# Splitting Q and K after the transpose, and the first projection in two passes

## What is computed

```python
def modulate(x, g, shift, scale):
    return rms_norm(x, g) * (1.0 + scale) + shift

sh1, sc1, gt1, sh2, sc2, gt2 = modulation(c, w_ada, b_ada)  # silu(c) @ w_ada + b_ada, in six parts
h = modulate(x, g_pre_attn, sh1, sc1)
qa, ka, va, qb, kb, vb = attn_projections(h, w_in, g_qa, g_ka)  # qa, ka normed per head
qa, ka = rope_2d(qa, rows, cols), rope_2d(ka, rows, cols)      # latent rows only
qb, kb = rope_2d(qb, rows, cols), rope_2d(kb, rows, cols)
oa = blocked_gqa(qa, ...)             # group A: 8 heads, 2 K/V heads, all keys
ob = windowed_gqa_with_ctx(qb, ...)   # group B: 8 heads, window of 128 and a sink
x = x + gt1 * rms_norm(concat(oa, ob) @ w_out, g_post_attn)
# then router, top-k per expert, 16 experts of SwiGLU, and the second residual
```

## Time and profile before

| | |
|---|---|
| median of 3 runs | 975.97 us (975.77 to 977.18) |
| the profiled execution | 975.98 us, span 974.2 us |
| PE busy | 902.5 us (93%) |
| DVE busy | 331.5 us (34%) |
| ACT busy | 214.8 us (22%) |
| POOL busy | 129.2 us (13%) |
| moved by DMA | 267.11 MB, mean 274 GB/s |

### The profile page before, as it was taken

One profiled execution on the slowest core, in us unless ns is written; L12 is line 12 of the kernel. 1 busy time (PEld: TensorE's weight loads), 2 busy tenths in 40 slices (PEclk: granted clock), 3 DMA queues, 4 the chain that ended last, 5 costly groups with the idle time before them and its releaser, 6 DMA issues.

```text
span 974.2 us, 20099 instructions
## 1 busy us (share of the span) xinstructions
PE 902.5 (93%) x8601; PEld 447.6 (46%) x8601; DVE 331.5 (34%) x872; ACT 214.8 (22%) x509; POOL 129.2 (13%) x226
## 2 busy tenths in 40 slices
PE   3899999899899999449999999999999999999996
PEld 2445545677656555314444444444444444444441
DVE  2355533888767763631111111101110111011016
ACT  5122212666644653200000000000000000000002
POOL 1101100000000000021212121212121212120121
PEclk9999999999999999759999999999999999999999
DMA  9997440400000006929999999999999999999973
GB/s 359 336 346 259 173 173 31 180 2 1 1 1 23 23 23 251 414 101 357 366 402 392 394 398 403 393 394 398 402 393 393 401 400 392 394 401 401 384 256 156
DMA packets 77813, 267.11 MB, mean 274 GB/s; under 512 B 6392, under 2 KB 12072, under 8 KB 77768
## 3 DMA queue, kind: packets, MB, share of 16 engines
q1 hardware_dynamic: 69040, 248.53, 65.3%
q0 software_dynamic: 7088, 14.95, 6.1%
q10 hardware_dynamic: 1640, 3.01, 0.8%
HBM read 252.32 MB, written 14.16 MB: 274 GB/s over the span
## 4 chain that ended last, share of the span: by engine, by line
PE 86%; DVE 6%; DMA 3%; ACT 3%; issue 2%; POOL 1%; SPq 0%; ACTq 0%; DVEq 0%
PE ps L835 34%; PE ps L847 17%; PE ps L553 11%; PE ps L707 6%; PE ps L658 3%; PE ps L636 3%; DMA ring<-in_w_ada 3%; PE ps L622 2%; PE ps L505 2%; PE ps L570 1%; ACT ring L1131 1%; PE ps L736 1%; PE ps L684 1%; PE ps L813 1%; PE ps L892 1%
## 5 line engine op out<-in xcount | busy, mean ns | idle before, releaser
L835 PE MATMUL ps<-ring,reg 128*32 128x512 f32 x2048 | 232.1, 593 | 0.0
L847 PE MATMUL ps<-ring,reg 128*32 128x256 f32 x2048 | 124.0, 383 | 3.2 <-DVE reg L1573 2.2
L835 PEld LDWEIGHTS ps<-ring,reg 128*32 128x32 f32 x2048 | 66.6, 110 | 126.9 <-issue 116.2
L553 PE MATMUL ps<-ring,reg_qt 128*128 128x512 f32 x240 | 105.7, 594 | 0.9 <-ACT reg_qt L981 0.9
L847 PEld LDWEIGHTS ps<-ring,reg 128*32 128x32 f32 x2048 | 65.9, 111 | 71.1 <-issue 34.0
L1177 ACT ACTIVATE reg<-ps 128x256 f32<-128x256 f32 x16 | 6.2, 385 | 390.0 <-PE ps L887 390.0
L1588 DVE TENSOR_SCALAR reg<-ps,kt 128x512 f32<-128x512 f32 x15 | 11.3, 751 | 214.4 <-PE ps L835 214.4
L707 PE MATMUL ps<-ring,reg 128*128 128x512 f32 x160 | 76.1, 603 | 0.0
L553 PEld LDWEIGHTS ps<-ring,reg_qt 128*128 128x128 f32 x240 | 44.5, 190 | 53.0 <-issue 51.2
L1131 ACT ACTIVATE ring<-ps 128x640 f32<-128x640 f32 (+3 forms) x80 | 44.4, 555 | 72.8 <-PE ps L636 69.8
L835 PE MATMUL ps<-reg_qt,kt 128*32 128x512 f32 x512 | 57.9, 592 | 0.0
(11 more groups left out here) (218 smaller groups left out, 1005.2 us busy)
## 6 DMA issues: line engine op xcount, KB each, us to landing
ring<-in_w_up SPq DMA_DIRECT2D x32, 2048.0 KB
ring<-in_w_down SPq DMA_DIRECT2D x32, 2048.0 KB
ring<-in_w_gate SPq DMA_DIRECT2D x16, 2048.0 KB
reg_qt<-in_w_gate SPq DMA_DIRECT2D x16, 2048.0 KB
ring<-in_w_ada SPq DMA_DIRECT2D x12, 2048.0 KB
reg<-in_x_sample SPq DMA_DIRECT2D x8, 512.0 KB, 6.0
ring<-in_w_in SPq DMA_DIRECT2D x2, 2048.0 KB
ring<-in_w_out SPq DMA_DIRECT2D x2, 2048.0 KB
```

The lines of the kernel that those rows point to most:

```text
L553: last = pe.matmul(ps[:, i % 2, :], hT[:, c, t * P:(t + 1) * P], w[:, c, :], start=(c == 0), stop=(c == KC - 1))
L835: last = pe.matmul(o[64 * n + r:64 * n + r + 32, :], x[:, j, hf, r:r + 32], w[:, j, n * HALF:(n + 1) * HALF], start=(hf == 0 and j == 0), ...
L847: last = pe.matmul(o[32 * q:32 * q + 32, :], x[:, c % 2, c // 2, :], w[:, j, q * QUART:(q + 1) * QUART], start=(c == 0), stop=(c == KC - 1))
```

## The change

Three things, all before the second unit of the attention.

1. **Split after the transpose.** `turn_qk(k)` transposes `rot` itself (queries) or `doubled` (keys, doubled by ACT in `double_keys`), four transposes into one bank. ACT's `high_part` takes the high part out of PSUM into its place in qT or kT, DVE's `low_part` subtracts that from PSUM into its place. For queries each takes two instructions over 64 partitions: the heads of a pair lie on partitions 0 to 63 and 64 to 127, and the low part goes to the other half.
2. **Shift and scale in column halves.** Units `half` hold 512 columns of all 1024 rows. `mod_half(i)` multiplies one (32 matmuls of 128 columns), `half_columns` transposes it, `half_cols` makes columns of it for four chunks.
3. **The first projection in two passes.** `project_half(t, b)` does four of the eight chunks, into five banks (`FIRST_BANKS`), one for each tile. DVE normalises x now, and the bias of shift and scale comes in four loads of its own.

```diff
-UNITS = ([("ada", m, h) for m in (0, 1) for h in (0, 1)] + [("win", 0, 0), ("win", 1, 0)]
+MOD_HALVES = [(m, a) for a in (0, 1) for m in (0, 1)]
+UNITS = ([("half", 0, 0), ("half", 1, 0), ("win", 0, 0), ("half", 0, 1), ("half", 1, 1), ("win", 1, 0)]
          + [("ada", m, h) for m in (2, 3) for h in (0, 1)] + [("ada", 4, 0), ("win", 2, 0)]
          + [("ada", 4, 1), ("ada", 5, 0), ("ada", 5, 1)] + [("wout", 0, h) for h in (0, 1)])
-UNIT_SLOT = [1, 2, 3, 4, 5, 0, 2, 3, 4, 2, 3, 5, 4, 2, 3, 4, 5]
+UNIT_SLOT = [1, 2, 5, 3, 4, 0, 2, 3, 4, 2, 3, 5, 4, 2, 3, 4, 5]
 ADA_AFTER = {4: 2, 7: 3, 9: 4, 12: 5}
-COLS = {0: 0, 1: 1, 3: 2, 4: 3}
+COLS = {3: 2, 4: 3}
+FIRST_BANKS = [0, 1, 2, 3, 5]
...
+        def turned(k):
+            return ps[:, (6 + k % 2) if k < 4 else (5 if k % 2 else 2), :]
...
+        def parts_of(k):
             s, t = divmod(k - 1, TILES)
-            if k == 0 or s == 0:
+            if k <= TILES:
+                at = KEY_AT[-1] if k == 0 else (TOK if t == 0 else KEY_AT[t - 1])
                 for g in (0, 1):
-                    if k == 0:
-                        src = cache[:, 2 * g * P:(2 * g + 1) * P]
-                    elif t == 0:
-                        src = kv_ctx[:, 256 * g:256 * g + P]
-                    else:
-                        src = rot[:, (k - 1) % 2, g * P:(g + 1) * P]
-                    dst = split[:, b, 512 * g:512 * g + 512].rearrange("p (v r u d) -> p r v u d", v=2, r=2, u=2)
-                    yield src.rearrange("p (v d) -> p v d", v=2).unsqueeze(2).to_broadcast([P, 2, 2, DH]), dst
+                    by_kv = kT[g][:, :, at:at + P].rearrange("p (v r) n -> p r v n", r=2)
+                    yield turned(k)[:, 256 * g:256 * g + 256].rearrange("p (v n) -> p v n", v=2), by_kv[:, 0], by_kv[:, 1]
             else:
-                yield (rot[:, (k - 1) % 2, :].rearrange("p (h d) -> p h d", d=DH),
-                       split[:, b, :].rearrange("p (h r d) -> p r h d", h=HEADS, r=2))
+                here, there = slice(0, DH), slice(DH, P)
+                by_pair = qT[s - 1][:, :, t * P:(t + 1) * P].rearrange("p (c r) n -> p r c n", r=2)
+                for r in (0, 1):
+                    yield (turned(k)[here].rearrange("p (c n) -> p c n", c=PAIRS), by_pair[here, r], by_pair[there, r])
+                    here, there = there, here
...
+                if kind == "half":
+                    freed.append((mod_half_done, MOD_HALVES.index((m, h)) + 1))
+                elif kind == "ada" and h == 0:
                     n_half += 1
                     freed.append((ada_half, n_half))
                 elif kind == "ada":
...
                     for t in range(TILES):
                         src = A["x_prompt"][0] if t == 0 else A["x_sample"][0, (t - 1) * P:t * P]
                         sp.dma_start(x_in[:, t, :], src).then_inc(x_loaded[t], 16)
-                if kind == "ada":
+                if kind == "half":
+                    src = A["w_ada"][0].rearrange("(p c) n -> p c n", c=KC)[:, :, m * D + HALF * h:m * D + HALF * (h + 1)]
+                    sp.dma_start(dst.rearrange("p (c n) -> p c n", c=KC), src).then_inc(slot_in[slot_of(u)], 16)
+                    if (m, h) == (1, 1):
+                        load_win0(1)
+                        load_keys()
...
+            def mod_half(i):
+                m, a = MOD_HALVES[i]
+                if i:
+                    pe.wait_ge(mod_ready, i)
+                u = UNITS.index(("half", m, a))
+                landed(u)
+                w = unit_at(u, KC)
+                for c in range(KC):
+                    for q in range(4):
+                        last = pe.matmul(ps[32 * q:32 * q + 32, 4, 0:P], silu[:, c, :], w[:, c, q * P:(q + 1) * P],
+                                         start=(c == 0), stop=(c == KC - 1))
+                last.then_inc(mod_half_done, 1)
...
-            ada(0)
-            mod_columns(0, 0)
-            ada(1)
-            mod_columns(1, 1)
+            mod_half(0)
+            turn_x(0)
+            turn_x(1)
+            half_columns(0)
+            turn_x(2)
+            turn_x(3)
+            mod_half(1)
+            turn_x(4)
+            half_columns(1)
+            turn_x(5)
...
+            def project_half(t, b):
+                if b == 0 and t == 1:
+                    pe.wait_ge(ht_ready, 4)
+                if b == 0 and t == 2:
+                    pe.wait_ge(ht_raw, KC)
+                    pe.wait_ge(htc_raw, KC)
+                if b == 1 and t == 1:
+                    pe.wait_ge(ht_ready, KC)
+                w = unit_at(win_units[0], KC)
+                for c in range(4 * b, 4 * b + 4):
+                    if t == 0:
+                        pe.wait_ge(htc_ready, c + 1)
+                        if c % 4 == 0:
+                            pe.wait_ge(win0_in[b], 32)
+                    last = pe.matmul(projected(t), hT[:, c, t * P:(t + 1) * P], w[:, c, :],
+                                     start=(c == 0), stop=(c == KC - 1))
+                if b:
+                    last.then_inc(proj_done, 1)
+            project_half(0, 0)
+            turn_x(6)
+            project_half(1, 0)
+            turn_x(7)
+            mod_half(2)
+            project_half(2, 0)
+            half_columns(2)
+            mod_half(3)
+            project_half(3, 0)
+            half_columns(3)
+            project_half(4, 0)
...
             def turn_qk(k):
-                pe.wait_ge(split_ready, k + 1)
-                if k < 2:
-                    pe.wait_ge(htc_ready, KC)
+                if k <= TILES:
+                    pe.wait_ge(doubled_ready, k + 1)
                 else:
+                    pe.wait_ge(rot_ready, k)
+                if k == 0:
+                    pe.wait_ge(htc_raw, KC)
+                    pe.wait_ge(modcol_ready, 4)
+                if k >= 2:
                     pe.wait_ge(qkT_ready, k - 1)
-                    pe.wait_ge(qkT_act, k - 1)
-                for b in range(8):
-                    last = pe.transpose(ps[:, turned_banks(k)[b // 4], (b % 4) * P:(b % 4 + 1) * P],
-                                        split[:, k % 2, b * P:(b + 1) * P], ident[:, :])
+                for b in range(4):
+                    src = doubled[:, k % 2, :] if k <= TILES else rot[:, (k - 1) % 2, :]
+                    last = pe.transpose(turned(k)[:, b * P:(b + 1) * P], src[:, b * P:(b + 1) * P], ident[:, :])
                 last.then_inc(qk_turned, 1)
...
+            for c in range(6):
+                copy_xc(c)
+            act.wait_ge(modcol_ready, 2)
+            for c in range(4):
+                modulate_xc(c)
+            copy_xc(6)
+            copy_xc(7)
+            act.wait_ge(modcol_ready, 4)
+            for c in range(4, KC):
+                modulate_xc(c)
+            def double_keys(k):
...
+            def high_part(k):
                 act.wait_ge(qk_turned, k + 1)
-                bank = ps[:, (5 if k % 2 else 2), :].rearrange("p (b n) -> p b n", b=4)
-                s, t = divmod(k - 1, TILES)
-                if k == 0 or s == 0:
-                    at = KEY_AT[-1] if k == 0 else (TOK if t == 0 else KEY_AT[t - 1])
-                    dst = kT[0][:, :, at:at + P]
-                else:
-                    if k == TILES + 1:
-                        act.wait_ge(added_l, 16)
-                        act.wait_ge(added_c, 16)
-                        act.wait_ge(pad_cleared, 16)
-                    dst = qT[s - 1][:, 0:4, t * P:(t + 1) * P]
-                act.activation(dst, bank, ACT.Copy).then_inc(qkT_act, 1)
+                if k == TILES + 1:
+                    act.wait_ge(added_l, 16)
+                    act.wait_ge(added_c, 16)
+                    act.wait_ge(pad_cleared, 16)
+                for src, high, low in parts_of(k):
+                    last = act.activation(high, src, ACT.Copy)
+                last.then_inc(qkT_act, 1)
...
+            add_bias(0)
+            copy_x(0)
+            copy_x(1)
+            half_cols(0)
+            copy_x(2)
+            copy_x(3)
+            add_bias(1)
+            copy_x(4)
+            half_cols(1)
             dve.wait_ge(modcol_ready, 2)
-            for c in range(KC):
-                dve.wait_ge(ht_raw, c + 1)
-                dve.tensor_scalar(hT[:, c, P:TOK], hT[:, c, P:TOK], cmod[:, 1, 1, c:c + 1], cmod[:, 0, 1, c:c + 1],
-                                  ALU.mult, ALU.add).then_inc(ht_ready, 1)
+            for c in range(4):
+                modulate_x(c)
...
-                dve.wait_ge(high_ready, k + 1)
-                for src, dst in part_sources(k):
-                    last = dve.tensor_tensor(dst[:, 1].bitcast(F32R), src, dst[:, 0], ALU.subtract)
-                last.then_inc(split_ready, 1)
-            def qk_out(k):
-                dve.wait_ge(qk_turned, k + 1)
-                bank = ps[:, (6 if k % 2 else 3), :].rearrange("p (b n) -> p b n", b=4)
-                s, t = divmod(k - 1, TILES)
-                if k == 0 or s == 0:
```

(13 more changed lines are left out.)

180 lines of the change are left out of this document (109 added, 71 removed).

## The result

The changed kernel takes **1042.7 us** (median of 4 runs, 1040.9 to 1044.1), the kernel before on the same chip 976.6 us (4 runs, 975.8 to 979.5). The ratio is 1.066, 95% interval 1.064 to 1.068: **6.6% slower**, where 970.6 us was forecast. Executions of one kernel differ with the clock granted to them: over all runs of before, those with a mean granted clock of 0.981 took 975.7 to 976.9 us, those with 0.976 or 0.977 took 977.1 to 980.3.

A forecast was written before the change was run, and what follows sets the result against it. TensorE was taken to bound the kernel, so gains before the attention sweep would reach the end one for one: 8.1 - 4.7 + 3.9 - 1.9 = 5.4 us less than 975.98, so 970.6 us, range 967.6 to 974.8.

The forecast's parts named there:

- T: The end of the last projection before attention, 166.56 us in the kernel before, forecast at 159.3.
- the tail: From the last projection into attention: pieces over 64 partitions delay the first turned probabilities, T+12.2 instead of T+10.37, 1.9 us lost.
- the sweep: The attention's 80 units, where PE, VectorE and ScalarE hand score blocks on; no gain or loss of its own was forecast.
- Startup: Before the first projection: with shift and scale in halves it starts at 27.8 instead of 35.91, 8.1 us earlier.
- Rivals A: Startup: a half of shift or scale costs what a whole does, 3.6 us; +5.9, 976.5 us, no change; chance 0.13.
- C: Startup: PE stays at 1.2 GHz through the first dense half projection; +7.7, 978.3 us; 0.07 together with D's late start.
- D: Startup: smaller ada pieces load slower, second half unit 1.7 us later; up to +1.5, 972.1 us; chance 0.07.
- The new wait: First projection's second passes: PE waits 0.7 us at turn_qk(3); with added work, 4.7 of 8.1 us given back by ada(2)'s end.
- The dense stretch: From 77.53 to 166.56 us, before attention: nine turn_qk each 0.44 us shorter, 3.9 us gained on PE.
- Rival B: Attention's first units catch up, so the 1.9 us lost on the way into attention vanish; 968.7 us; chance 0.11.

The follow-up runs named there:

- after_plus24: The changed kernel with 24 more PE instructions (empty semaphore waits) ahead of its first matmul: 974.35 us, 0.9963 of the kernel before.
- after_plus72: The changed kernel with 72 already satisfied waits ahead of its first modulation half: 973.4 us, 0.9959 of the kernel before.
- split_plus24: The kernel before with only the split after the transpose, plus 24 instructions of waits to place the loop: 976.97 us, 0.9991 of the kernel before.
- tail_plus24: The changed kernel with 24 instructions of waits, last two turned tiles in banks 6 and 7, their low parts subtracted later: 969.1 us, 0.9907 of the kernel before.

## Why the prediction was wrong

**The step that failed** is in the first paragraph: "the expert loop is paced by PE, so what is won or lost before the sweep should reach the end one for one", and "the expert loop unchanged". The work in it is unchanged, its place in the program is not. I counted what the change adds and removes in time, on each engine, and never in instructions. Nothing in the page of before warned of it: 76 instructions of room were left to the limit, 131 were added, and a loop that fits shows no trace of the limit but packets that are missing.

The rest of the miss is in the sum itself: in the profiled execution T is 7.50 us earlier (7.3 forecast), the tail gives back 2.8 (1.9) and the sweep 1.0 (nothing), which is the 3.65 at the loop instead of 5.4.

The steps one by one:

- **Startup: right.** mod_half(0) starts at 16.87 (16.7) and takes 3.64 (4.2, at half speed), the next half 1.96 (2.2), the first projection starts at 27.94 (27.8). Rows of after:

```profile
16.87 3.64 PE L536 MATMUL ps<-ring,reg 128*32 128x128 f32 x64 [16.87 <-DMA ring<-in_w_ada]
...
23.84 1.96 PE L536 MATMUL ps<-ring,reg 128*32 128x128 f32 x64
...
27.94 3.70 PE L609 MATMUL ps<-ring,reg_qt 128*128 128x512 f32 x8 [0.79 <-ACT reg_qt L1059]
```

  Rivals A (halves at 3.6 us), C (the clock low until the first projection) and D (smaller pieces slower) fall by these rows: the pace rises between the 3.64 and the 1.96 of the same 64 instructions, though the granted clock reads 1.00 in both. The rule of the Trainium skill ("TensorE: Matmul & The Clock Gate", Part 3, The mechanism) that was weighed against the row gave an estimate of 3.5 us a half; 1.96 was measured, so at this shape a load does not add up with its matmul.
- **The new wait: right, and its place.** turn_qk(3) waits 0.44 us (0.7), the only one of the second passes; ada(2) ends at 73.95 (74.1).

```profile
69.78 0.66 PE L649 MATMUL ps<-ident,reg 128*128 128x128 f32 x4 [0.44 <-ACT reg L1082]
70.36 3.66 PE L557 MATMUL ps<-ring,reg 128*32 128x256 f32 x64
73.95 7.13 PE L633 MATMUL ps<-ring,reg_qt 128*128 128x512 f32 x16
80.92 0.60 PE L649 MATMUL ps<-ident,reg 128*128 128x128 f32 x4
```

- **The dense stretch: right.** turn_qk takes 0.44 us less (0.60 to 1.04), T is 159.06 (159.3).
- **The tail: right mechanism, too small.** 2.8 us and not 1.9. Two pieces over 64 partitions take 1.39 us on VectorE and 1.18 on ScalarE, where about 1.2 and 1.1 were taken; the prediction's own price for them in the dense stretch, twice 0.68, was the better one. VectorE works without a wait from the first of these subtractions, and the first maximum starts at T + 7.6, not T + 7.0; the second exponential ends at T + 10.3, not T + 9.8. Rival B falls too: the sweep catches nothing up.
- **The sweep: not in the sum.** From turn_probs(0) to the routing after takes 1.0 us more than before, after_plus24 4.1, after_plus72 3.9, split_plus24 3.4. Each has a stretch of low granted clock that before lacks (160 to 180 us in all four), after_plus24 for one:

```profile
160.00:170.00 10.00, 4.26 (x16) 3.16 (x14) 8.33 (x19) 5.37 (x10) 0.00 (x0) 0.65 0.62 229
170.00:180.00 10.00, 8.62 (x56) 7.71 (x56) 8.21 (x21) 4.93 (x10) 0.00 (x0) 0.66 0.73 272
...
260.00:270.00 10.00, 10.00 (x29) 5.41 (x29) 6.32 (x24) 3.62 (x13) 0.00 (x0) 0.73 0.00 0
```

  after has the same waits of PE ahead of 260 and no fall there; tail_plus24 has none either. **What decides between them stays open.** The executions compared are not alike either: the trace of after_plus24 is of its longest of ten (976.60 us against a median of 974.35, mean granted clock 0.965 against 0.970 to 0.976), and its loop starts at 430.13, level with before, whose trace is of one with 0.981. So the gain of after_plus24 stands in its median and not in its trace.

So with its loop in place the change is worth 0.4%: 972.0 to 972.4 us, 1.4 to 1.8 over the forecast and inside its range. As it was written it costs 6.6%.

## What to carry to other kernels

Before a change ahead of a long loop, count instructions as well as time: where in its block the loop's first instruction falls, how far its last one reaches, and how many more the change puts ahead. A loop that turns slow while its own code is the same, with waits that nothing ends ("issue") just behind the jump and packets on the instruction queue in each round, is such a case, and a few idle instructions ahead of it are test and cure in one. And a tail that hands tiles over between engines is settled by the order on the engine that sets the pace, not by the free bank alone.

## What the runs showed of the hardware

- A loop of PE's program whose last instruction was the 1788th from the start of its first block of 256 jumped back with no instruction packet from 510 to 860 us (977.7 us in all); one that reached the 1796th, four past 7 x 256, was fetched again at every jump. That is 9 packets of 16 KB a jump, two waits (3.79 and 4.35 us at the first jump of after), and 61 to 68 us for six jumps.
- The transfers of the weights fall back behind PE's waits: after moved 291 GB/s from 515 to 520 us and 31 from 520 to 525, and 350 over 430 to 940 us, where before moved 384. SP's waits there are for PE's products, which free its slots. Whether full DMA queues lengthen the fetch was not tried.
- 168 waits in a row that were satisfied already held PE up by 6.70 us, about 0.04 us a wait, 0.08 an instruction.
- PE's granted clock fell between 160 and 180 us behind a wait of 4.5 us (to 0.75 and 0.74 in after, 0.65 and 0.66 in after_plus24), and still fell (0.76 and 0.90) with the waits cut to 2.94 and 1.09; it kept 1.00 with these filled down to 0.75 and 0.54.
